# The second LayerNorm of a decoder layer: tile one is normalised before tile two's second half of statistics

## The reference, cut to what matters

```python
x = layer_norm(DN_ALPHA * x + merged @ w_o[i], ln1_g[i], ln1_b[i])
y_m = hier_moe(x, ...)                       # 64 experts, top 2 of one group
x = layer_norm(DN_ALPHA * x + y_m, ln2_g[i], ln2_b[i])      # the second norm
ple = sigmoid(x @ w_ple_gate[i] + b_ple_gate[i]) * (p[i] @ w_ple_up[i])
x = layer_norm(DN_ALPHA * x + ple, ln3_g[i], ln3_b[i])
```

## Time and profile before

| what | value |
|---|---|
| median of 3 runs | 1567.45 us (1562.42 to 1567.77) |
| the profiled execution, its own time | 1564.71 us |
| its span, first to last instruction | 1563.0 us |
| mean granted TensorE clock | 0.923 of full |
| busy time of TensorE matmuls, of the span | 1300.6 us (83%) |
| busy time of VectorE | 412.9 us (26%) |
| busy time of ScalarE, GpSimd | 202.7 us (13%), 36.9 us (2%) |

### The profile page before, as it was taken

One profiled execution on the slowest core, in us unless ns is written; L12 is line 12 of the kernel. 1 busy time (PEld: TensorE's weight loads), 2 busy tenths in 40 slices (PEclk: granted clock), 3 DMA queues, 4 the chain that ended last, 5 costly groups with the idle time before them and its releaser, 6 DMA issues.

```text
span 1563.0 us, 21663 instructions
## 1 busy us (share of the span) xinstructions
PE 1300.6 (83%) x8737; PEld 730.0 (47%) x8737; DVE 412.9 (26%) x815; ACT 202.7 (13%) x407; POOL 36.9 (2%) x94
## 2 busy tenths in 40 slices
PE   9999999996576677578999999999867748757787
PEld 4686444553233434234466854446534425423433
DVE  4244442511010011111633464344101101101126
ACT  2311000211010000000213120003101100000011
POOL 2000000100000000000100000001000000000000
PEclk9999999998788889889999999999978879978898
DMA  9733467499999999999674344647999999999990
GB/s 317 263 108 109 162 256 307 175 425 425 426 427 424 425 424 426 426 426 418 233 276 162 108 154 167 256 203 293 424 426 427 426 425 422 425 426 426 427 391 27
DMA packets 105225, 503.87 MB, mean 322 GB/s; under 512 B 15154, under 2 KB 18244, under 8 KB 55108
## 3 DMA queue, kind: packets, MB, share of 16 engines
q1 hardware_dynamic: 104564, 501.85, 79.7%
q10 hardware_dynamic: 592, 1.06, 0.2%
HBM read 501.83 MB, written 1.05 MB: 322 GB/s over the span
## 4 chain that ended last, share of the span: by engine, by line
PE 57%; DMA 37%; DVE 2%; issue 2%; ACT 1%; SPq 1%; ACTq 0%; POOLq 0%; DVEq 0%; POOL 0%
DMA ring<-in_w_down 36%; PE ps L1195 11%; PE ps L990 9%; PE ps L687 7%; PE ps L757 7%; PE ps L1037 5%; PE ps L702 5%; PE ps L1159 3%; PE ps L1144 3%; PE ps L1208 1%; SPq L512 1%; DMA ring<-in_w_in 1%; PE ps L740 1%; PE ps L1089 0%; PE ps L1290 0%
## 5 line engine op out<-in xcount | busy, mean ns | idle before, releaser
L1195 PE MATMUL ps<-ring,pads 128*32 128x512 f32 x384 | 165.2, 817 | 110.2 <-DMA ring<-in_w_down 110.2
L1195 PE MATMUL ps<-scratch,pads 128*32 128x512 f32 x512 | 165.2, 787 | 85.7 <-DMA ring<-in_w_down 85.6
L1159 PE MATMUL ps<-ring,pads 128*32 128x256 f32 x2560 | 227.0, 379 | 0.0
L1159 PEld LDWEIGHTS ps<-ring,pads 128*32 128x32 f32 x2560 | 123.4, 110 | 74.1 <-issue 11.6
L1144 PEld LDWEIGHTS ps<-pads,xT 128*128 128x128 f32 x1024 | 122.6, 197 | 25.4 <-issue 25.4
L1144 PE MATMUL ps<-pads,xT 128*128 128x128 f32 x1024 | 123.6, 280 | 9.1 <-issue 9.1
L1208 PE MATMUL ps<-mats,pads 128*128 128x512 f32 x256 | 118.3, 605 | 2.4 <-ACT mats L1470 2.4
L1159 PE MATMUL ps<-scratch,pads 128*32 128x256 f32 x1536 | 116.2, 379 | 3.3 <-ACT pads L1458 3.3
L2021 DVE COPY mats<-ps 128x512 f32<-128x512 f32 x32 | 22.1, 692 | 349.5 <-PE ps L1195 349.5
L1195 PEld LDWEIGHTS ps<-ring,pads 128*32 128x32 f32 x384 | 37.7, 145 | 164.3 <-issue 122.5
L757 PE MATMUL ps<-ring,xT 128*128 128x512 f32 x256 | 111.7, 592 | 0.0
(11 more groups left out here) (281 smaller groups left out, 1206.3 us busy)
## 6 DMA issues: line engine op xcount, KB each, us to landing
ring<-in_w_up SPq DMA_DIRECT2D x128, 1024.0 KB, 26.1
scratch<-in_w_gate SPq DMA_DIRECT2D x96, 1024.0 KB, 25.7
scratch<-in_w_down SPq DMA_DIRECT2D x64, 1024.0 KB, 21.5
ring<-in_w_in SPq DMA_DIRECT2D x48, 1024.0 KB, 7.2
ring<-in_w_down SPq DMA_DIRECT2D x48, 1024.0 KB, 23.1
ring<-in_w_gate SPq DMA_DIRECT2D x32, 1024.0 KB, 25.9
x<-in_w_down SPq DMA_DIRECT2D x16, 1024.0 KB, 26.2
ring<-in_w_br SPq DMA_DIRECT2D x12, 1024.0 KB, 6.2
```

The costliest lines, as they stand in the source:

```text
L1159: ins = mm(ps[32 * j:32 * j + 32, 2, i * 256:i * 256 + 256], xgT[:, k, 32 * j:32 * j + 32], w[j][:, k, :], start=(k == 0), stop=(k == K - 1))
L1195: ins = mm(ps[32 * j:32 * j + 32, n, :], hT[:, cc, 32 * j:32 * j + 32], w[j][:, cc, n * 512:n * 512 + 512], start=(cc == 0), stop=(cc == 1))
```

## The change

Nothing is added or removed; VectorE's instructions of this stage are put in another order. Before: statistics of tile one (two halves), moments of tile one, statistics of tile two (two halves), moments of tile two, normalise tile one, normalise tile two, `xT_high` of tile one, `xT_high` of tile two. After: statistics and moments of tile one, first half of tile two's statistics, normalise tile one, second half of tile two's statistics, moments of tile two, `xT_high` of tile one, normalise tile two, `xT_high` of tile two. The other engines' programs stay as they are.

```diff
-                for t in range(T):
-                    wait_full(dve, f"acc{t}", L)
-                    for h in range(2):
-                        link(dve.bn_stats(st6[:, t, h, :], half(f"acc{t}", h)))
-                    moments(t)
-                for t in range(T):
+                def acc_stats(t, h):
+                    link(dve.bn_stats(st6[:, t, h, :], half(f"acc{t}", h)))
+                def acc_normalise(t):
                     dve.wait_ge(power_out, power(L, "ln2", t))
                     ins = dve.tensor_scalar(x[:, t, :], pair(f"acc{t}"), mv[:, t, 0:1], rstd[:, t:t + 1],
                                             ALU.subtract, ALU.mult)
                     ins.then_inc(x_ready, 1)
                     dve.wait_ge(x_ready, xT_turn(L, 2, t) + 1)
                     dve.sem_inc(free[job(f"acc{t}")[0]], 1)
-                for t in range(T):
-                    xT_high("x2T", L, t, vecT[:, 33:49])
+                wait_full(dve, "acc0", L)
+                acc_stats(0, 0)
+                acc_stats(0, 1)
+                moments(0)
+                wait_full(dve, "acc1", L)
+                acc_stats(1, 0)
+                acc_normalise(0)
+                acc_stats(1, 1)
+                moments(1)
+                xT_high("x2T", L, 0, vecT[:, 33:49])
+                acc_normalise(1)
+                xT_high("x2T", L, 1, vecT[:, 33:49])
```

## The result

Over 20 runs of each kernel, taken in turns, the changed kernel's median is 1570.09 us and that of before 1564.62 us; the ratio is 1.0036, with a 95% interval of 1.0028 to 1.0044. The change costs 5.6 us (4.4 to 6.9). Two single executions further down, 2689.26 us in e8 and 1766.26 us in e12, ran in a far slower state and are left out of the ratios.

What follows compares the result with a forecast made beforehand. It took the end of tile two's normalisation, which frees `acc1`'s port for TensorE, as the bound; 2 x 2.55 = 5.1 us plus 1.66 us for one clock fall, 6.8 us on 1567.45, gave 1574.2 us, range 1570.0 to 1578.0.

Steps and rivals of the forecast that it cites:

- Tile one's normalisation and the transposes: Second norm's stage: tile one's normalisation starts 0.62 us earlier, TensorE's transposes stay put, gain 0 us.
- `xT_high` in front of tile two's normalisation, and the port: VectorE waits for tile one's transposes, so `acc1` is freed late and `ple_up(1, 0)` waits: 2.55 us a layer.
- the 0.10 us in front of `pg00`: TensorE's small gap between `ple_up(1, 0)` and `pg00`, claimed to vanish after the change.
- The cost of the split statistics: Tile two's second half of statistics (0.72 us), moments (0.2 us) and GpSimd's power, claimed hidden.
- The clock: TensorE's clock falls behind the new 2.87 us pause, chance 0.55 a layer, 1.66 us for each fall.
- The sum's clock term: One clock fall over the two layers counted in the forecast, 1.66 us.
- Both falls: Rival: clock falls behind the pause in both layers; 8.4 us slower, 1575.9 us; chance 0.28.
- No fall: Rival: clock falls behind the pause in neither layer; 5.1 us slower, 1572.6 us; chance 0.24.
- No stall: Rival: tile one's `xT_high` on VectorE would not wait for transposes; 0.6 us gain, 1566.8 us; chance 0.04.
- The first layer's delay swallowed by the experts: Rival: second layer's expert transfers hide the first layer's 2.55 us; about 2.6 us slower, 1570.1 us; chance 0.06.

Runs made afterwards that it cites:

- e8: Changed kernel with three matmuls without use behind tile one's transposes, run a second time; ratio to before 1.0020.
- e12: Kernel before with two matmuls without use instead of one in each layer's router wait, run a second time; 1562.68 us, ratio to before 0.9987.
- filled pause: Changed kernel with three matmuls without use on TensorE behind tile one's transposes; ratios to before 1.0015 and 1.0020.
- e1: Kernel before with only tile one's `xT_high` moved between the two normalisations; ratio to before 1.0037.
- e5: Changed kernel with `ple_up(1, 0)` moved behind tile two's transposes in the middle of `pg00`; ratio to before 1.0018, 2.8 us.
- e3: Changed kernel with three matmuls without use behind tile one's transposes, first run; ratio to before 1.0015.
- e2: Changed kernel with tile two's normalisation put back in front of tile one's `xT_high`; ratio to before 1.0014, 2.2 us.
- the router filled: Two matmuls without use instead of one in each layer's router wait; kernel before 1562.56 and 1562.68 us, changed kernel 1571.16 us.
- e10: Changed kernel with two matmuls without use instead of one in each layer's router wait; 1571.16 us, ratio to before 1.0037.
- e4: Changed kernel, unaltered, run again for another profile; ratio to before 1.0039.
- e9: Changed kernel, unaltered, run again for a further profile; ratio to before 1.0041.

## Why the prediction was right, point by point

**Tile one's normalisation and the transposes.** Right. It starts 4.75 us behind `combine`'s start (1514.32 - 1509.57), forecast 4.68; the transposes did not move.

**`xT_high` in front of tile two's normalisation, and the port.** Right: 2.55 us a layer forecast, 2.55 us measured by the filled pause (idle 2.77 us in the changed kernel, forecast 2.87), and e1 and e5 show both links of it, the order on VectorE and the port of `pu1`. That the hundredths agree is luck: VectorE's four instructions overlap the normalisation by 0.09 us, a bound that the prediction named, and the 0.10 us in front of `pg00` did not vanish as it said (1.82 us from line 1290 to line 757 in e3, as in before). The cost of the split statistics was called hidden, and it is, but only under this larger wait; e2 shows 1.44 us of it when that cover is taken away.

**The clock.** The price was right, 1.66 us forecast, 1.5 to 1.7 us measured. The chance was not: I gave the fall 0.55 a layer and summed one; it came ten times in ten. The sum's clock term should have been 3.3 us, and the change 8.4 us. That 6.8 us is nearer to the measured 5.6 us (4.4 to 6.9) than 8.4 is luck. The prediction took the kernel around the stage as fixed, though its own rows show a fall that came at one router and not at the other: falls at the routers and in the experts' last groups come and go from execution to execution, by up to 1.7 us at a router and 2.9 us in a last group. In the two profiles compared above they took 5.9 us in before and nothing in the changed kernel, which is why those two are only 2.2 us apart.

**The rivals.** Both falls: they came, but with 5.6 us and not 8.4, which is what they cost only with the router filled. No fall: out. No stall: out. The first layer's delay swallowed by the experts: out, by e10 and by the constant 315.8 and 428.4 to 428.8 us. What stays open is why, by the medians, 2.6 us of the stages' 8.25 are missing in the changed kernel, and 2 to 3 us of 5.1 in the filled one (e3, e8). Since the profiles differ nowhere else by more than a few tenths, e3 and e4 excepted, fewer or shorter falls at the routers and in the last groups are the likely place. But whether the change makes them rarer is not shown: e4 and e10 have a fall in both last groups, and the changed kernel and e9 lack them in the first layer's last group too, which runs before any edited stage.

## What to carry to other kernels

When an instruction is moved forward on an in-order engine, ask what now stands behind the wait that it brings along: the early piece was worth nothing since its reader was busy, and the late piece held a buffer that the reader needed next. Ask also whether a small step on another engine, here GpSimd's power, was covered by the work that is moved away. And price a new pause of TensorE as the pause plus a clock fall behind it. Before comparing two profiles of single executions, add up the clock falls outside the edited place: here they differed by 5.9 us, as much as the whole change.

## What the runs showed of the hardware

A pause of TensorE of 2.77 us behind eight transposes was followed by the lower clock in ten places out of ten, at a price of 1.5 to 1.7 us; pauses of 1.64 us (e2) and 1.63 us (e5) in the same place were not, four out of four, with a granted clock of 1.00 behind them. Three matmuls without use in the pause, 2.74 us, kept the clock at full in all six places, though the wait stayed as long. At the routers and in the experts' last groups, where TensorE was busy 2.37 of 3.70 us and 0.88 of 4.00 us just before, the clock fell in some executions and not in others.
